# Gated linear attention started within its gates' projection, dilated attention within its values, and the stick's vector work reordered

## The chip, the cores and the metric

The kernel runs on one core of a Trainium2 chip. The metric is the time of one execution on the device, in microseconds (us). TensorE (PE) multiplies matrices; VectorE (DVE), ScalarE (ACT) and GpSimd (POOL) do everything else on tiles; SyncE (SP) and POOL start transfers. Each engine takes its instructions from a queue of its own, in a fixed order, and an instruction that waits for a semaphore holds up all that stand behind it in that queue.

## The reference

Two transformer blocks follow each other on one sequence of 512 tokens with 1024 features, all in float32. Block 1 normalises, projects with `w_in`, runs two mixers, joins them with `w_out`, and ends in a squared-relu MLP. One mixer is gated linear attention (GLA, 4 heads):

```python
glog = log_sigmoid(glow @ gla_gate_w2 + gla_gate_b) / 16
b = cumsum(glog, within chunks)                    # per channel
o = gated linear attention(q, k, v, b)             # exp(b), exp(-b) scale q and k
o_a = rmsnorm_per_head(o) * silu(gr)               # gr: the gates' projection
```

The other is dilated attention, 8 heads: softmax of `q.k + bias` over three dilated windows, joined by their log-sum-exp, times the values. Block 2 has stick-breaking attention (8 heads) and HGRN2 (4 heads of 128) side by side, then gated branches, an output projection and a SwiGLU:

```python
sp = where(causal, softplus(z), 0)                 # z = q.k / 8
w = exp(log_sigmoid(z) - (reverse cumsum(sp) - sp))
o_sb = w @ v
f = lb + (1 - lb) * sigmoid(f_in); log_f = log(f); key = 1 - f     # HGRN2
q = silu(q_in); out = hgrn2(q, key, i_in, log_f) * silu(g_in)
```

## The kernel before

Every large product is computed from split operands: a high and a low part of each (names ending in H and L: NH, NL, WH, WL), and three matmuls of 128x512 for each step over k: high by high (L660), low by high (L664), high by low (L667). One such step is called a unit here. Weights come as 128x1024 pieces into a ring of five (WH, WL): ACT rounds a piece to its high part (L1030), ACT writes the negative of that (L1038), and a transfer issued by POOL adds the raw weights to it (L2191).

The program is written as generators, one set for each engine, that yield a due time ahead of each instruction or small group. The due times are in units of PE's plan (`plan.start("qD")` is the place at which the projection qD starts); for each engine all generators are merged by due time, once, into that engine's queue. At run time only the order is left; the times themselves delay nothing.

The stages in plan order, with what matters here: the projections qG, kG, vG; the four tiles of the gate projection gG (8 units each); then the projections qD, kD, vD of dilated attention; wo0 and wo1, the two halves of `w_out`; the MLP; and in block 2 hq, hf, vH, hg, the four projections of HGRN2, beside the stick.

What the change touches:

- **GLA** (`gla` on every engine, due times from `gla_time`, which counts from `T_D`). It runs in two chunks of two heads, c=0 and c=1. PE multiplies the low-rank gate (L756); ACT takes the bank (L1099) and does abs, exp and ln (L1102, L1104, L1106); DVE finishes the logarithm (L1584) and makes three cumulative sums over 64, 128 and 256 columns (L1588, L1590, L1593); ACT takes exponentials (L1111, L1112), DVE multiplies q and k by them (L1596, L1598), and PE multiplies those (L766, a block of 16 small matmuls). Then, for 64, 128 and 256 in turn, DVE subtracts (L1604, `decay`), ACT takes two exponentials (L1116, L1117) and DVE multiplies (L1608, L1610, `values`) for PE's L777, L787 and L793. DVE masks (L1626) and PE multiplies by the values (L813).
- **The gates gG** (`silu_gates` on ACT, `silu_gate` on DVE). For each tile DVE takes it out of its bank with a scale (L1562, here called the eviction), ACT does abs, exp, ln (L954, L956, L958), DVE a step (L962), ACT an exp (L966), DVE the product (L1567). The two temporaries gT0 and gT1 take turns, and GLA's `decay` uses the same two.
- **Dilated attention** (`dilated`, due times from `T_A1` and the step `R1`). In 12 steps PE multiplies q and k (L858), DVE adds the bias and takes the row maximum (L1706), ACT takes exponentials with a sum (L1152), DVE divides (L1688, L1693), PE transposes (L846), ACT copies the bank (L1164, tile pT), and PE multiplies by the values (L833). The values' tiles of vD are taken out of their banks by ACT (L1073).
- **The stick** (`stick`, two of eight heads p=0, 1 in each step). DVE does a softplus part (L1725), the reverse scan (L1730), a difference (L1734), and for the next step a masked copy (L1746) and an abs (L1752); ACT does exp and ln (L1191, L1198, L1202) and copies the transposed weights (L1184, tile wT) for PE's L833.
- **HGRN2's gates** beside the stick: hf has the same chain as gG and ends in L1914 and L1916 on DVE and a logarithm (L1277) on ACT. `calm` gives their due times within the stick's step. vH's tiles are taken out by ACT (L1073).

## Time and profile before

| | |
|---|---|
| median of 3 runs | 1362.75 us (1362.65 to 1363.94) |
| the profiled execution | 1364.07 us |
| its span, first to last instruction | 1362.7 us |
| PE busy | 1348.6 us, 99% of the span |
| DVE busy | 873.2 us, 64% |
| ACT busy | 819.9 us, 60% |

The span is what the rows below are told in, from its start. The profiled execution is 1.3 us above the median and has 1.4 us outside its span. A busy time is the time in which an engine worked on some instruction; idle time of an engine costs only where the last engine to finish waits for it.

### The profile page before, as it was taken

Reading aid. Unit: us, or ns where it says so; the run is one execution under the profiler, and the core shown is the slowest. Engines: PE = TensorE matmul, PEld = TensorE weight load, DVE = VectorE, ACT = ScalarE, POOL = GpSimd, SP = SyncE. Lnnn points to the kernel's source line nnn. Section 1 sums busy time; section 2 is a strip of 40 time slices with the busy share of each in tenths; the row PEclk is TensorE's granted clock in tenths of the full one; section 3 lists DMA queues with packets and bytes.
Section 4 is the critical chain, followed back from the end, with each engine's and each line's share of the span. In section 5 each row is a group of like instructions: output and inputs, shape, how many; then the busy total and the mean of one; then the engine's idle time right before and its main releaser. Section 6 shows DMA issues by size and latency. Waiting matters only on the chain.

```text
span 1362.7 us, 19539 instructions
## 1 busy us (share of the span) xinstructions
PE 1348.6 (99%) x7510; PEld 1135.7 (83%) x7510; DVE 873.2 (64%) x1548; ACT 819.9 (60%) x1235; POOL 334.6 (25%) x306
## 2 busy tenths in 40 slices
PE   9999999999999999999999999999999999999999
PEld 6977956789899898887777788888888898889889
DVE  6055466577576682357787779975437785568557
ACT  6575566753544545666577767775666645754553
POOL 0211101235343251111211121211113252315214
DMA  7976643925436137876654685668888536824733
GB/s 251 238 165 144 148 117 78 231 32 196 99 98 179 33 125 191 193 169 144 149 129 111 137 217 125 137 145 182 201 214 203 110 118 194 184 47 164 188 51 109
DMA packets 57969, 202.45 MB, mean 149 GB/s; under 512 B 6450, under 2 KB 7019, under 8 KB 57748
## 3 DMA queue, kind: packets, MB, share of 16 engines
q0 software_dynamic: 25632, 93.09, 36.4%
q1 hardware_dynamic: 31380, 106.24, 23.7%
q10 hardware_dynamic: 864, 1.87, 0.4%
q8 instruction: 60, 0.98, 0.3%
q14 instruction: 33, 0.27, 0.1%
HBM read 199.05 MB, written 2.12 MB: 148 GB/s over the span
## 4 chain that ended last, share of the span: by engine, by line
PE 77%; DVE 11%; ACT 8%; DMA 3%; issue 2%; SPq 0%; POOL 0%; DVEq 0%; ACTq 0%
PE bank L660 18%; PE bank L667 18%; PE bank L664 18%; PE bank L698 17%; DVE eb L1730 2%; PE bank L813 1%; ACT WL L1038 1%; ACT eb L1198 1%; ACT WH L1030 1%; ACT zs L1152 1%; PE bank L885 1%; DVE eb L1725 1%; DMA WL<-in_w_in 1%; DMA WL<-in_w_gu 1%; DMA RAW<-in_w_in 1%
## 5 line engine op out<-in xcount | busy, mean ns | idle before, releaser
L660 PE MATMUL bank<-NH,WH 128*128 128x512 f32 x1152 | 459.8, 400 | 0.3 <-ACT NH L1207 0.3
L664 PE MATMUL bank<-NL,WH 128*128 128x512 f32 x1152 | 448.1, 390 | 0.6 <-DVE NL L1470 0.5
L667 PE MATMUL bank<-NH,WL 128*128 128x512 f32 x1152 | 448.1, 390 | 0.6 <-DVE WL L1465 0.4
L660 PEld LDWEIGHTS bank<-NH,WH 128*128 128x128 f32 x1152 | 216.5, 188 | 60.2 <-issue 17.8
L667 PEld LDWEIGHTS bank<-NH,WL 128*128 128x128 f32 x1152 | 216.2, 188 | 47.5 <-DVE WL L1465 0.8
L664 PEld LDWEIGHTS bank<-NL,WH 128*128 128x128 f32 x1152 | 216.8, 188 | 44.7 <-DVE NL L1470 1.6
L1030 ACT ACTIVATE WH<-RAW 128x1024 fp32r<-128x1024 f32 (+3 forms) x148 | 152.1, 1032 | 74.4 <-PE bank L667 39.0
L698 PE MATMUL bank<-AH,WH 128*128 128x256 f32 x644 | 182.5, 283 | 0.3 <-DVE AL L2115 0.3
L698 PE MATMUL bank<-AL,WH 128*128 128x256 f32 x644 | 182.2, 283 | 0.0
L698 PE MATMUL bank<-AH,WL 128*128 128x256 f32 x644 | 182.2, 283 | 0.0
L1038 ACT ACTIVATE WL<-WH 128x1024 fp32r<-128x1024 f32 (+1 forms) x146 | 153.3, 1052 | 12.2 <-DMA WH<-in_w_in 9.9
L2191 POOL DMA_DIRECT2D WL<-in_w_in x58 | 50.9, 889 | 318.2 <-ACT WL L1038 314.8
L698 PEld LDWEIGHTS bank<-AH,WH 128*128 128x128 f32 x644 | 123.6, 192 | 0.9 <-ACT AH L1381 0.4
L698 PEld LDWEIGHTS bank<-AL,WH 128*128 128x128 f32 x644 | 123.6, 192 | 0.2
L698 PEld LDWEIGHTS bank<-AH,WL 128*128 128x128 f32 x644 | 123.6, 192 | 0.0
L2203 POOL TENSOR_TENSOR quarters<-quarters 128x512 f32<-128x512 f32 (+1 forms) x48 | 72.2, 1503 | 128.4 <-PE bank L667 60.3
L2203 POOL TENSOR_TENSOR quarters_s<-quarters 128x512 f32<-128x512 f32 (+1 forms) x48 | 78.8, 1641 | 97.0 <-PE bank L667 51.2
L1025 ACT ACTIVATE WH<-quarters 128x1024 fp32r<-128x1024 f32 (+3 forms) x72 | 62.4, 883 | 65.0 <-PE bank L698 45.4
L1819 DVE TENSOR_TENSOR WL<-quarters,WH 128x1024 fp32r<-128x1024 f32 (+3 forms) x72 | 86.9, 1208 | 6.7 <-ACT WH L1025 6.7
L660 PE MATMUL bank<-WH,NH 128*128 128x256 f32 (+2 forms) x224 | 67.4, 308 | 2.9 <-ACT vH L1073 2.6
L1849 DVE TENSOR_TENSOR gains_hT<-gains_hT,bank 128x256 f32<-128x256 f32 x143 | 58.2, 414 | 16.2 <-PE bank L698 15.9
L667 PE MATMUL bank<-WL,NH 128*128 128x256 f32 (+2 forms) x224 | 65.1, 299 | 0.3 <-DMA WL<-in_w_in 0.3
(375 smaller groups left out, 2115.3 us busy)
## 6 DMA issues: line engine op xcount, KB each, us to landing
WL<-in_w_in POOLq DMA_DIRECT2D x58, 512.0 KB, 7.2
RAW<-in_w_gu SPq DMA_DIRECT2D x44, 512.0 KB, 5.1
WL<-in_w_gu POOLq DMA_DIRECT2D x34, 512.0 KB, 8.0
RAW<-in_w_ff SPq DMA_DIRECT2D x32, 512.0 KB, 4.6
WH<-in_w_in POOLq DMA_DIRECT2D x32, 512.0 KB, 7.1
RAW<-in_w_in SPq DMA_DIRECT2D x28, 512.0 KB, 6.4
quarters<-in_w_ff SPq DMA_DIRECT2D x24, 512.0 KB, 4.7
WL<-in_w_ff POOLq DMA_DIRECT2D x17, 512.0 KB, 6.5
```

The source lines that it names most:

```text
L660: e.matmul(o, a[0], a[1], start=(k == 0), stop=False)
L664: e.matmul(o, b[0], b[1], start=False, stop=False)
L667: mm = e.matmul(o, c[0], c[1], start=False, stop=(k == t.kt - 1))
L698: mm = e.matmul(o, a, b, start=(n in OPENS and j == 0 and i == 0), stop=(n in CLOSES and j == pairs_ - 1 and i == 2), skip_group_check=True)
L1025: e.activation(WH[p % HL][:, 0:(c if k == 3 else 2 * c)], part, ACT.Copy).then_inc(*act.sig("high", p))
L1030: e.activation(WH[p % HL][:, 0:n], RAW[raw_slot[p]][:, 0:n], ACT.Copy).then_inc(*act.sig("high", p))
L1038: e.activation(WL[p % HL][:, 0:n], WH[p % HL][:, 0:n].bitcast(F32), ACT.Copy, scale=-1.0).then_inc(*act.sig("high_negated", p))
L1730: scan = e.tensor_tensor_scan(r, r, r, 0.0, ALU.add, ALU.max)
L1819: e.tensor_tensor(WL[(p + i) % HL][:, 0:n], x, WH[(p + i) % HL][:, 0:n].bitcast(F32), ALU.subtract).then_inc(*dve.sig("low_sum", p + i))
L1849: e.tensor_tensor(hT[:, row, ts], hT[:, row, ts], bank, ALU.add).then_inc(*dve.sig("h_part", u, n))
L2191: e.dma_start(WL[p % HL][:, 0:n], src[:, k * cols:(k + m) * cols], accum_op=ALU.add).then_inc(*pool.sig(f"low_added{p % HL}", p, by=16))
L2203: e.tensor_tensor(to, a, b, op).then_inc(*pool.sig("quarter_sum", u, key))
```

## The change

It has four parts. `T_D` is 12 units earlier, so that GLA begins in the middle of gG; the gates' temporaries are then two rows of `mixed` which dilated attention fills later, and GLA's two waits for the gates are gone. `T_A1` is 4 units earlier and `R1` is 2.4 in place of 2.13, so that dilated attention begins within vD and ends where it did. In the stick each head's scan is followed at once by its difference, and each masked copy by its abs. The products of HGRN2's gates get later due times, 11.3 and 11.5 in place of 9 and 9.2 (hg: 11).

```diff
--- before.py
+++ after.py
@@ -496,8 +496,8 @@
 
             return s % 2 if bank == 0 else bank + 1
 
-        T_D = plan.start("qD")
-        T_A1, R1 = plan.start("wo0"), 3 * 0.71
+        T_D, W0 = plan.start("qD") - 12.0, plan.start("wo0")
+        T_A1, R1 = W0 - 4.0, 2.4
         T_A2, R2 = plan.start("hq") - 10.0, 4 * 2.3
         T_H, R3 = plan.start("gs"), 3.5
         ORDER = [(hp, rows) for hp in range(4) for rows in (((0, 0), (1, P)), ((2, 0),), ((3, 0),))]
@@ -548,7 +548,7 @@
             if p in after:
                 return seven_start(plan.first[after[p][0]]) + (3.0, 4.4, 12.8, 17.5, 20.2)[after[p][1]]
 
-            return plan.used[p - HL] + (1.3 if plan.used[p - HL] == T_A1 else 0.1)
+            return plan.used[p - HL] + (1.3 if plan.used[p - HL] == W0 else 0.1)
 
         def seven_start(p):
             return next(t.v0 for t in plan.tiles if t.u == plan.pieces[p][0])
@@ -1064,7 +1064,7 @@
 
             def natural(st, v, ph):
                 for t in plan.stage[st]:
-                    yield max(t.v1 + (1.4 if t.v1 == T_A1 else 1), ready_columns[ph])
+                    yield max(t.v1 + (1.4 if t.v1 == W0 else 1), ready_columns[ph])
                     j, c, bank = t.i % NT, t.i // NT, bank_for(t)
                     act.wait_ge(("product", "tile", t.g), ("scale_columns", ph))
                     if st == "vS" or st == "vH":
@@ -1272,7 +1272,7 @@
                     sigmoid_act(("hf", t.i), hk[:, t.i, :], hs[t.i % 2], freed(t), *hs_back("hf", t.i))
                     yield calm(t, 7.0)
                     sigmoid_exp(("hf", t.i), hs[t.i % 2])
-                    yield calm(t, 9.2)
+                    yield calm(t, 11.5)
                     act.wait_ge(("hf_f", t.i))
                     e.activation(hB[:, t.i, :], hs[t.i % 2], ACT.Ln).then_inc(*act.sig("hf_log", t.i))
                 return [one_(t) for t in plan.stage["hf"]]
@@ -1396,9 +1396,10 @@
 
             streams = [prologue(), ones(), splits(), negated(), root("attn", mean_time["attn"]), columns("attn", 30.0)]
             streams += [natural("vG", vG, "attn"), natural("vD", vD, "attn")]
-            streams += silu_gates("gG", lambda i: mixed[:, i, :], gt_, lambda i: [("gate", "gG", i - 2)] if i >= 2 else [])
+            streams += silu_gates("gG", lambda i: mixed[:, i, :], [mixed[:, 4, :], mixed[:, 5, :]],
+                                  lambda i: [("gate", "gG", i - 2)] if i >= 2 else [("band", i)])
             streams += [gla(0), gla(1)]
-            streams += [mixed_split("mixed", k, T_A1 - 2.0 + 0.2 * k, [("gla_out", k), ("product", "block", plan.last_unit("vD"), k)])
+            streams += [mixed_split("mixed", k, W0 - 2.0 + 0.2 * k, [("gla_out", k), ("product", "block", plan.last_unit("vD"), k)])
                         for k in range(4)]
             streams += [dilated()]
             streams += [mixed_split("mixed", k, dil_done(k - 4), [("dil_out", k - 4)]) for k in range(4, 8)]
@@ -1562,7 +1563,7 @@
                     e.tensor_tensor(o, bank_for(t), rs, ALU.mult).then_inc(*dve.sig("evac_v", t.g))
                     yield calm(t, 6.0)
                     sigmoid_dve((st, t.i), o, x)
-                    yield calm(t, 11.0 if st == "hg" else 9.0)
+                    yield calm(t, 9.0 if st == "gG" else 11.3)
                     dve.wait_ge(("sigmoid", (st, t.i)), ("evac_v", t.g))
                     e.scalar_tensor_tensor(o, o, gain(t.i), x, ALU.mult, ALU.mult).then_inc(*dve.sig("gate", st, t.i))
                 return [one_(t) for t in plan.stage[st]]
@@ -1610,11 +1611,11 @@
                     e.tensor_tensor(halves(x, m)[1], halves(d, m)[1], halves(qc, m)[1], ALU.mult).then_inc(*dve.sig("gla_x", c, m, 1))
 
                 yield gla_time(c, 5) + 0.1
-                decay(64, B64, d0, [("gla_out", 1)] if c else [("gate", "gG", 2)])
+                decay(64, B64, d0, [("gla_out", 1)] if c else [])
                 yield gla_time(c, 6)
                 values(64, d0, x64, [("gla_64", 0, 1)] if c else [])
                 yield gla_time(c, 7) + 0.1
-                decay(128, B128, d1, [] if c else [("gate", "gG", 3)])
+                decay(128, B128, d1, [])
                 yield gla_time(c, 8)
                 values(128, d1, x128_, [("gla_128", 0, 1)] if c else [])
                 dve.wait_ge(("gla_x", c, 64, 1))
@@ -1729,7 +1730,6 @@
                                 r = ee[p][:, at_:at_ + (i + 1) * P][:, ::-1]
                                 scan = e.tensor_tensor_scan(r, r, r, 0.0, ALU.add, ALU.max)
                             scan.then_inc(*dve.sig("stick_sum", s - 1, p))
-                        for p in range(2):
                             dve.wait_ge(("stick_sum", s - 1, p))
                             e.tensor_tensor(z[p], z[p], ee[p], ALU.subtract).then_inc(*dve.sig("stick_log", s - 1, p))
                     if s < NA:
@@ -1745,7 +1745,6 @@
                                 w = slice(at_, at_ + (i + 1) * P)
                                 low_ = e.tensor_tensor(z[p][:, w], FB[p][:, w], gmask[:, (3 - i) * P:S], ALU.min)
                             low_.then_inc(*dve.sig("stick_b", s, p))
-                        for p in range(2):
                             dve.wait_ge(("stick_b", s, p))
                             if s:
                                 dve.wait_ge(("stick_log", s - 1, p))
@@ -1909,7 +1908,7 @@
                     e.tensor_tensor(o, bank_for(t), rs, ALU.mult).then_inc(*dve.sig("evac_v", t.g))
                     yield calm(t, 6.0)
                     sigmoid_dve(("hf", t.i), o, f)
-                    yield calm(t, 9.0)
+                    yield calm(t, 11.3)
                     dve.wait_ge(("sigmoid", ("hf", t.i)), ("lb", 6))
                     e.tensor_scalar(f, f, olb[:, t.i:t.i + 1], lb[:, t.i:t.i + 1], ALU.mult, ALU.add).then_inc(*dve.sig("hf_f", t.i))
                     dve.wait_ge(("hf_f", t.i))
@@ -2141,9 +2140,10 @@
 
             streams = [prologue(), early_low(), sums("attn"), root("attn", mean_time["attn"]), bands(), low_rank()]
             streams += [put("qG", qG, 0.125), put("kG", kG)]
-            streams += silu_gate("gG", lambda i: mixed[:, i, :], lambda i: g_gla[:, i:i + 1], gt_, [])
+            streams += silu_gate("gG", lambda i: mixed[:, i, :], lambda i: g_gla[:, i:i + 1],
+                                 [mixed[:, 4, :], mixed[:, 5, :]], [])
             streams += [gla(0), gla(1), put("qD", qD, 0.125), put("kD", kD)]
-            streams += [mixed_split("mixed", k, T_A1 - 2.0 + 0.2 * k, []) for k in range(4)]
+            streams += [mixed_split("mixed", k, W0 - 2.0 + 0.2 * k, []) for k in range(4)]
             streams += [dilated(), to_h("wo0", "wo0", lambda k: x_in(k)[-1])]
             streams += [mixed_split("mixed", k, dil_done(k - 4), []) for k in range(4, 8)]
             streams += [to_h("wo1", "mlp", lambda k: ("h", "wo0", k)), sums("mlp")]
```

In the following pieces of the queues a line number of the changed kernel is one higher than that of the same line before, between 1400 and 1733, and one lower from 1749 on. gB and gX hold GLA's sums and products, mixed1 the gates.

DVE, from the second gate tile on, before:

```order
L962 SCALAR_TENSOR_TENSOR gT1_102<-mixed1_76,gT1_102 128x512 [waits sigmoid_a]
L1567 SCALAR_TENSOR_TENSOR mixed1_76<-mixed1_76,gains_hT_51,gT1_102 128x512 [waits evac_v,sigmoid]
L1562 TENSOR_TENSOR mixed1_76<-bank1,rs_69 128x512 [waits product]
L962 SCALAR_TENSOR_TENSOR gT0_101<-mixed1_76,gT0_101 128x512 [waits sigmoid_a]
L1581 MEMSET AT0_103 128x512 [waits masks]
L1581 MEMSET AT1_104 128x512
L1567 SCALAR_TENSOR_TENSOR mixed1_76<-mixed1_76,gains_hT_51,gT0_101 128x512 [waits evac_v,sigmoid]
L1562 TENSOR_TENSOR mixed1_76<-bank2,rs_69 128x512 [waits product]
L1584 SCALAR_TENSOR_TENSOR gB0_97<-gB0_97,gB1_98 128x512 [waits gla_a]
L1588 SCALAR_TENSOR_TENSOR gB2_99<-resets_73,gB0_97 128x512 [waits gla_vector]
L1590 SCALAR_TENSOR_TENSOR gB3_100<-resets_73,gB0_97 128x512
L1593 SCALAR_TENSOR_TENSOR gB0_97<-resets_73,gB0_97 128x512 [waits gla_vector]
```

and changed:

```order
L1563 TENSOR_TENSOR mixed1_76<-bank0,rs_69 128x512 [waits product]
L1582 MEMSET AT0_103 128x512 [waits masks]
L1582 MEMSET AT1_104 128x512
L1585 SCALAR_TENSOR_TENSOR gB0_97<-gB0_97,gB1_98 128x512 [waits gla_a]
L1589 SCALAR_TENSOR_TENSOR gB2_99<-resets_73,gB0_97 128x512 [waits gla_vector]
L962 SCALAR_TENSOR_TENSOR mixed1_76<-mixed1_76 128x512 [waits sigmoid_a]
L1591 SCALAR_TENSOR_TENSOR gB3_100<-resets_73,gB0_97 128x512
L1594 SCALAR_TENSOR_TENSOR gB0_97<-resets_73,gB0_97 128x512 [waits gla_vector]
L1568 SCALAR_TENSOR_TENSOR mixed1_76<-mixed1_76,gains_hT_51 128x512 [waits evac_v,sigmoid]
L1563 TENSOR_TENSOR mixed1_76<-bank1,rs_69 128x512 [waits product]
L1597 TENSOR_TENSOR gX0_92<-qG_80,gX0_92 128x512 [waits gla_a]
L1599 TENSOR_TENSOR gX1_93<-kG_81,gX1_93 128x512 [waits gla_a]
```

GLA's logarithm and first sum have moved ahead of the second tile's L962, and the second tile's product and the third tile's eviction now stand between GLA's sums and its products with q and k.

ACT, from GLA's bank on, before:

```order
L1099 ACTIVATE gB0_97<-bank4,gains_hT_51 128x512 [waits gla_products]
L1102 ACTIVATE gB1_98<-gB0_97 128x512 [waits gla_a]
L1104 ACTIVATE gB1_98<-gB1_98 128x512 [waits gla_a]
L1106 ACTIVATE gB1_98<-gB1_98 128x512 [waits gla_a]
L1038 ACTIVATE WL0_57<-WH0_52 128x1024 [waits high]
L954 ACTIVATE gT1_102<-mixed1_76 128x512 [waits gate,evac_v]
L956 ACTIVATE gT1_102<-gT1_102 128x512 [waits sigmoid_a]
L958 ACTIVATE gT1_102<-gT1_102 128x512 [waits sigmoid_a]
L1111 ACTIVATE gX0_92<-gB2_99 128x512 [waits gla_vector]
L1112 ACTIVATE gX1_93<-gB2_99 128x512
```

and changed:

```order
L1099 ACTIVATE gB0_97<-bank4,gains_hT_51 128x512 [waits gla_products]
L1102 ACTIVATE gB1_98<-gB0_97 128x512 [waits gla_a]
L1104 ACTIVATE gB1_98<-gB1_98 128x512 [waits gla_a]
L1106 ACTIVATE gB1_98<-gB1_98 128x512 [waits gla_a]
L966 ACTIVATE mixed1_76<-mixed1_76 128x512 [waits sigmoid_v]
L954 ACTIVATE mixed1_76<-mixed1_76 128x512 [waits gate,evac_v]
L956 ACTIVATE mixed1_76<-mixed1_76 128x512 [waits sigmoid_a]
L958 ACTIVATE mixed1_76<-mixed1_76 128x512 [waits sigmoid_a]
L1111 ACTIVATE gX0_92<-gB2_99 128x512 [waits gla_vector]
L1112 ACTIVATE gX1_93<-gB2_99 128x512
```

The second tile's exp and the whole abs, exp and ln of the third tile, which waits for that tile's eviction on DVE, now stand between GLA's logarithm and its exponentials L1111.

ACT, the exponentials of the three differences, before:

```order
L966 ACTIVATE gT1_102<-gT1_102 128x512 [waits sigmoid_v]
L1116 ACTIVATE gT0_101<-gB2_99 128x4x64 [waits gla_vector]
L1117 ACTIVATE gT0_101<-gT0_101 128x4x64
L1116 ACTIVATE gT1_102<-gB3_100 128x2x128 [waits gla_vector]
L1117 ACTIVATE gT1_102<-gT1_102 128x2x128
L1030 ACTIVATE WH1_53<-RAW1_63 128x1024 [waits product,raw1]
L1116 ACTIVATE gT0_101<-gB0_97 128x256 [waits gla_vector]
L1117 ACTIVATE gT0_101<-gT0_101 128x256
```

and changed:

```order
L1116 ACTIVATE gT0_101<-gB2_99 128x4x64 [waits gla_vector]
L1117 ACTIVATE gT0_101<-gT0_101 128x4x64
L1030 ACTIVATE WH4_56<-RAW2_64 128x1024 [waits product,raw2]
L1038 ACTIVATE WL4_61<-WH4_56 128x1024 [waits high]
L1116 ACTIVATE gT1_102<-gB3_100 128x2x128 [waits gla_vector]
L1117 ACTIVATE gT1_102<-gT1_102 128x2x128
L966 ACTIVATE mixed1_76<-mixed1_76 128x512 [waits sigmoid_v]
L1030 ACTIVATE WH0_52<-RAW0_62 128x1024 [waits product,raw0]
L1116 ACTIVATE gT0_101<-gB0_97 128x256 [waits gla_vector]
L1117 ACTIVATE gT0_101<-gT0_101 128x256
```

Two weight pieces and the third tile's exp now stand among them, one piece before the second pair, one and a half around the third.

DVE in one step of the stick, next to the first tile of hf (hs0), before:

```order
L1752 SCALAR_TENSOR_TENSOR eb0_139<-zb0_136 128x384 [waits stick_log,stick_b]
L1752 SCALAR_TENSOR_TENSOR eb1_140<-zb1_137 128x384 [waits stick_log,stick_b]
L1914 TENSOR_SCALAR hs0_143<-hs0_143,small_49 128x512 [waits constants,sigmoid]
L1916 TENSOR_SCALAR hk_147<-hs0_143 128x512 [waits hf_f]
L1725 SCALAR_TENSOR_TENSOR eb0_139<-zb0_136,eb0_139 128x384 [waits stick_l]
L1725 SCALAR_TENSOR_TENSOR eb1_140<-zb1_137,eb1_140 128x384 [waits stick_l]
L1730 SCALAR_TENSOR_TENSOR eb0_139<-eb0_139 128x128 [waits stick_sp]
L1730 SCALAR_TENSOR_TENSOR eb0_139<-eb0_139 128x256
L1730 SCALAR_TENSOR_TENSOR eb1_140<-eb1_140 128x128 [waits stick_sp]
L1730 SCALAR_TENSOR_TENSOR eb1_140<-eb1_140 128x256
L1734 TENSOR_TENSOR zb0_136<-zb0_136,eb0_139 128x384 [waits stick_sum]
L1734 TENSOR_TENSOR zb1_137<-zb1_137,eb1_140 128x384 [waits stick_sum]
```

and changed:

```order
L1746 TENSOR_TENSOR zb1_137<-bank4,cf_67 128x128 [waits stick_t,stick_z]
L1746 TENSOR_TENSOR zb1_137<-bank4,cf_67 128x256
L1751 SCALAR_TENSOR_TENSOR eb1_140<-zb1_137 128x384 [waits stick_log,stick_b]
L1726 SCALAR_TENSOR_TENSOR eb0_139<-zb0_136,eb0_139 128x384 [waits stick_l]
L1726 SCALAR_TENSOR_TENSOR eb1_140<-zb1_137,eb1_140 128x384 [waits stick_l]
L1731 SCALAR_TENSOR_TENSOR eb0_139<-eb0_139 128x128 [waits stick_sp]
L1731 SCALAR_TENSOR_TENSOR eb0_139<-eb0_139 128x256
L1734 TENSOR_TENSOR zb0_136<-zb0_136,eb0_139 128x384 [waits stick_sum]
L1731 SCALAR_TENSOR_TENSOR eb1_140<-eb1_140 128x128 [waits stick_sp]
L1731 SCALAR_TENSOR_TENSOR eb1_140<-eb1_140 128x256
L1734 TENSOR_TENSOR zb1_137<-zb1_137,eb1_140 128x384 [waits stick_sum]
L1913 TENSOR_SCALAR hs0_143<-hs0_143,small_49 128x512 [waits constants,sigmoid]
```

hf's two instructions (L1914 and L1916 before, L1913 and L1915 now) have moved from ahead of the softplus part to behind the differences, and each head's difference stands behind its own scan.

## Rows read from the trace of the kernel before

**Rows 1.** Busy time by engine, whole span: us, share, instructions.

```profile
PE 1348.6 (99%) x7510; PEld 1135.7 (83%) x7510; DVE 873.2 (64%) x1548; ACT 819.9 (60%) x1235; POOL 334.6 (25%) x306
```

**Rows 2.** Waits of PE by line and releaser: us in total, times, longest us.

```profile
PE bank L660 <- ACT vH L1073: 2.6, 4, 1.3
PE bank L846 <- DVE zs L1693: 1.6, 2, 1.1
...
PE bank L833 <- ACT wT L1184: 1.2, 1, 1.2
PE bank L858 <- DVE small L1706: 1.0, 2, 0.6
...
PE bank L833 <- ACT pT L1164: 0.6, 3, 0.3
```

**Rows 3.** Three windows: us, busy us of each engine, clock, DMA share, GB/s.

```profile
80.00:104.00 24.00, 24.00 (x130) 18.19 (x130) 14.01 (x25) 15.98 (x29) 2.94 (x4) 1.00 0.70 157
172.00:230.00 58.00, 54.63 (x376) 34.76 (x374) 37.32 (x136) 38.31 (x101) 3.46 (x4) 1.00 0.41 96
664.00:780.00 116.00, 111.96 (x703) 86.49 (x702) 91.71 (x169) 84.05 (x155) 20.95 (x29) 1.00 0.59 133
```

**Rows 4.** Timeline of PE, first GLA chunk: start us, us, instruction.

```profile
71.49 0.39 PE L660 MATMUL bank<-NH,WH 128*128 128x512 f32 x1
...
79.43 0.39 PE L667 MATMUL bank<-NH,WL 128*128 128x512 f32 x1
79.75 1.12 PE L756 MATMUL bank<-glT,gw 16*128 16x512 f32 x2
...
91.22 1.16 PE L766 MATMUL bank<-gX,gX 64*128 64x128 f32 x16
...
96.38 1.03 PE L793 MATMUL bank<-gX 64*128 64x256 f32 x4
```

**Rows 5.** Timeline of ACT in the same stretch.

```profile
73.12 0.64 ACT L966 ACTIVATE gT<-gT 128x512 f32<-128x512 f32 x1 [0.76 <-DVE gT L962]
75.17 0.63 ACT L954 ACTIVATE gT<-mixed 128x512 f32<-128x512 f32 x1 [1.42 <-DVE mixed L1562]
...
77.04 1.05 ACT L1030 ACTIVATE WH<-RAW 128x1024 fp32r<-128x1024 f32 x1
...
80.90 0.69 ACT L1099 ACTIVATE gB<-bank,gains_hT 128x512 f32<-128x512 f32 x1 [0.25 <-PE bank L756]
...
82.96 0.63 ACT L1106 ACTIVATE gB<-gB 128x512 f32<-128x512 f32 x1
...
86.29 0.62 ACT L1111 ACTIVATE gX<-gB 128x512 f32<-128x512 f32 x1
```

**Rows 6.** Timeline of DVE in the same stretch.

```profile
72.39 0.69 DVE L962 SCALAR_TENSOR_TENSOR gT<-mixed,gT 128x512 f32<-128x512 f32 x1 [2.70 <-ACT gT L958]
73.79 0.75 DVE L1567 SCALAR_TENSOR_TENSOR mixed<-mixed,gains_hT,gT 128x512 f32<-128x512 f32 x1 [0.70 <-ACT gT L966]
74.46 0.68 DVE L1562 TENSOR_TENSOR mixed<-bank,rs 128x512 f32<-128x512 f32 x1
...
83.62 0.69 DVE L1584 SCALAR_TENSOR_TENSOR gB<-gB,gB 128x512 f32<-128x512 f32 x1 [2.54 <-ACT gB L1106]
84.35 1.23 DVE L1588 TENSOR_TENSOR_SCAN gB<-resets,gB 128x512 f32<-128x512 uint8 x1
...
89.06 0.68 DVE L1598 TENSOR_TENSOR gX<-kG,gX 128x512 f32<-128x512 f32 x1
...
94.15 1.35 DVE L1626 COPY_PREDICATED AT<-resets,bank 128x512 f32<-128x512 uint8 x2
...
95.72 0.42 DVE L1610 TENSOR_TENSOR gX<-gT,qG 128x256 f32<-128x256 f32 x1
```

**Rows 7.** Timeline of DVE, the stick beside hf.

```profile
730.06 0.55 DVE L1914 TENSOR_SCALAR hs<-hs,small 128x512 f32<-128x512 f32 x1 [1.94 <-ACT hs L966]
```

**Rows 8.** Timeline of ACT, the same step.

```profile
732.13 1.06 ACT L1184 ACTIVATE wT<-bank 128x512 f32<-128x512 f32 x2
```

## Prediction

> **What bounds the kernel now.** First the busy times: PE works 1348.6 us, 99% of the span [rows 1]. The instructions of the change are the same in number and kind on every engine, so PE's own work stays as it is, and the time can change only by the 14 us in which PE stands still. Then PE's waits, grouped by what released them [rows 2]: of these stops, three kinds are those of dilated attention (zs 1.6, small 1.0, pT 0.6, together 3.2 us) and two are those of the stick beside HGRN2's projections (vH 2.6, wT 1.2, together 3.8 us). No row there names a GLA product of DVE. Then the windows [rows 3]: in the one in which GLA's first chunk runs, 80 to 104 us, PE is busy 24.00 of 24.00; dilated attention has 3.4 us of idle in 58, the stick's window 4.0 in 116; PE's clock is 1.00 in all three. So the change can win at most some 7 us in the second and third window, and in the first it can only lose. How much slack the first has is read from the timelines.
>
> **GLA's first chunk, step by step.** Before, L756 starts at 79.75 and L766, which needs the two products with q and k, at 91.22; the second product ends on DVE at 89.06 + 0.68 = 89.74 [rows 4, 6]. So 1.5 us of slack. L793 starts at 96.38, and its operand is ready at 95.72 + 0.42 = 96.14: 0.2 to 0.4 us of slack. The chain is nearly as long as the room that PE gives it.
>
> In the changed queue of PE L756 stands 36 matmuls earlier; the 36 in front of it begin at 71.49 and end with the one at 79.43, so 8.2 us [rows 4]. L756 would start at 71.6, and without stops L766 at 83.0 to 83.1, as far behind as before. Then:
>
> ACT takes the bank 1.15 us after L756 (80.90 less 79.75), at 72.7, and begins L1106 2.06 later at 74.8 [rows 5]. DVE follows 0.66 later at 75.45, and the first sum at 76.2 (84.35 less 83.62 is 0.73) [rows 6]. Up to 75.45 DVE's queue stands at GLA's logarithm. Behind it stands the second gate tile's L962, which ran at 72.39 before; it now runs at 77.3, behind the first sum (1.14 a sum with the overlap). Two more sums bring DVE to about 80.2, the second tile's product (0.67 to the next start) to 80.9, and the third tile's eviction, at 74.46 before, to 81.6 [rows 6]. Here the convoy forms: ACT's queue has that tile's abs, exp and ln ahead of GLA's two exponentials, and they can't start until 81.6. Three at 0.66 end at 83.5, the two exponentials at 84.7, and DVE's two products at 85.45. PE would want L766 at 83.1: a stop of **2.4 us**. GLA's own chain would have been ready: its first sum is there at 77.4.
>
> The same holds behind it. From L766 at 85.5 L793 is due 5.16 later (96.38 less 91.22), at 90.7. On ACT the first pair of exponentials ends at 86.6; then a weight piece rounded and negated, some 2.05 (one takes 1.05 [rows 5]), the second pair 0.8, the gate tile's exp 0.55, another piece's rounding 1.05, and the third pair 0.75: 91.8. DVE runs the tile's product, the next eviction (0.65 each) and two masks, 1.24 together from 94.15 to the next start [rows 6], after its third difference at 90.1, and has them behind it at 92.7 to 92.9; the last two products take 0.75, so 93.5 to 93.7. The stop is **2.8 us**. Both are read from fixed queues, but each waiting adds some error: 1.5 to 3.2 and 1 to 3.5.
>
> The second chunk begins within kD. No gate tile stands in it, only two evictions of 0.68 and three weight instructions of 1.05 in front of its last products. I take 0.7 (0, if its slack covers them, to 2.8, the first chunk's). Three of the L813 blocks wait for a DVE chain into which an eviction slips: 0.2 each, 0.6 (0 to 1). GLA in all: 2.4 + 2.8 + 0.7 + 0.6 = **+6.5 us**, 3 to 9.
>
> The removed waits for the gates and the separate temporaries take nothing from this: the queues' order makes the gates' work a neighbour of GLA's, whatever rows it uses. A weight piece that ACT treats 9.5 us later (L1030 at 77.04 before [rows 5], at 86.6 now) I price at nothing: it goes into a ring of five, a full round ahead of its use, and the stops above give 5 us of the 9.5 back; uncovered, PE would stop for the other 4. On SP the bias tables of dilated attention now stand ahead of two loads of raw weights; the transfer engines are busy 0.41 to 0.70 of these windows [rows 3], so this is priced at nothing too.
>
> **Dilated attention.** It begins 4 units earlier and each of the steps is 0.27 units wider, some 0.2 us of PE between the same work. The first transposes still wait for the first softmax (of the zs waits, 1.1 is one stop), since the work put ahead of them moves too: 1.1 stays. The first product with the values now has a weight piece (1.05) and the last eviction of vD in front of its copy on ACT: from a short wait to about 1.5, which is new 1.2. The later stops, 3.2 - 1.1 = 2.1, and a short one of 0.2 at the stage's start go with the wider steps. That would be -2.3 + 1.2 = **-1.1 us**, from -2.5 (nothing new) to +1 (the later stops half stay).
>
> **The stick.** Before, DVE stands idle 1.94 us in front of hf's L1914, which waits for ACT's L966, while the softplus part is queued behind it [rows 7]. The changed order puts the stick's part first. On ACT the logarithm leaves the place in front of a weight piece, so wT's copy, at 732.13 [rows 8], comes 1.0 earlier: of the 1.2 that PE waits for it 0.2 is left. Of vH's 2.6 [rows 2] three stops are large; two hang on the same DVE wait, one step later, and shrink by what DVE stood idle; the middle one is set by ACT's own row of ln, exp, weight piece, eviction, which is unchanged, and keeps most of its 0.5 idle. I leave 1.3 of 3.8: **-2.3 us** net of 0.2 for the next item, from -3.8 to -0.5, since ACT's eviction of vH stays behind the same exponentials.
>
> The turned pairs make each head's difference wait for its own scan. A dependent instruction begins 0.04 after the end of the one in front (84.35 against 83.62 + 0.69), an independent one 0.08 before it (74.46 against 73.79 + 0.75) [rows 6]: 0.12 each, two in each half step for the second head, while the first head's result is out a scan earlier. If every half step in which PE stops paid it, five, it would be 5 x 0.24 = 1.2; I take 0.2. The Trainium skill, "VectorE: DVE Perf Modes", section "The DRAIN you can't avoid", says that chained vector instructions cost the same with a semaphore after each as with one at the end, since the pipe empties in any case. By that the item would be 0 and the sum 0.2 lower; the rows just named differ by 0.12, and the measurement decides.
>
> **The sum.** +6.5 - 1.1 - 2.3 = +3.1 against the profiled execution's 1364.07: 1367.2. That execution lies 1.3 above the median of the runs, so the median becomes 1365.9.
>
> **Rivals.**
>
> *Covered start.* The gates' steps find DVE and ACT free between GLA's, because in 80 to 104 us DVE is busy only 14.0 and ACT 16.0 of 24 [rows 3], and PE keeps its 24.00 of 24.00. Decided at L766: it starts within 0.5 us of its due place. Then GLA costs 0 to 0.5, the two gains stand, and the median is 1362.75 - 3.4 + 0.3 = 1359.7: faster. Against it: the slack of 1.5 and 0.3 us and the order of the queues. The Trainium skill, "Perfetto Trace Analysis", section "Optimization Strategy", says that stages bound by different engines may gain from being interleaved. That speaks for this rival; but here the rows show PE full in the stage that is interleaved.
>
> *Half a convoy.* The first stop comes, 2.4, but it gives the later pieces room: the weight pieces don't hold the last exponentials, the second chunk is covered. GLA +3.3, sum -0.1: 1362.7, no change. For it: DVE and ACT both catch up while PE stands. Against it: L793's slack before was the smallest.
>
> *The gains don't come.* The stick's stops belong to ACT (both lines, vH and wT, are ACT's [rows 2]), and what DVE does earlier ACT does no earlier; dilated attention's stops move to its start. Sum +6.5 at most: 1369.2. For it: the releasers' names; against it: ACT's own wait for hf's product.
>
> **How the numbers follow.** The forecast as summed has 0.50, 1364.0 to 1367.8 on its own; half a convoy 0.22; covered start 0.12; no gains 0.16. A difference of 0.2%, 2.7 us, is about what a measurement of this kernel tells from none: faster is below 1360.0, slower above 1365.5. Covered start and a little of half a convoy give faster 0.13. The forecast lies 0.4 above the upper bound, so three fifths of its 0.50 are slower, with the last rival 0.46; the rest, 0.41, is no change. The range, 1361.0 to 1369.2, leaves out covered start and the upper part of the last rival.
>
> **What would show it.** In the changed profile L766 of the first chunk follows its L756 by some 13.9 us in place of 11.5, PE waits there for DVE's gX, and DVE idles some 5 us in front of the first GLA logarithm with the gate's L962 behind it; L793 of that chunk waits as well. In the window of dilated attention one stop at L833 near the start has grown and the later ones are gone. In the stick's window DVE no longer idles 1.9 us in front of hf's product and wT's wait is about 0.2. If L766 doesn't wait, the forecast is wrong in its largest term; if PE's idle in the stick's window stays near 4.0, in its second.

## The result, and the profile after

The changed kernel takes 1368.39 us (median of 12 runs, 1367.30 to 1375.37), before 1363.87 in as many: ratio 1.0042, 95% interval 1.0031 to 1.0052. It is slower, as forecast, by 4.5 us against before's 12 runs; the sum had +3.1, and it stood on the median of the three runs shown, 1362.75, 1.1 below the one of twelve. The mean granted clock is 0.993 to 0.999 in all 12 runs of the changed kernel; for before it is on record for the profiled execution and for the 59 runs beside the experiments, 1.000 in each. The profiled execution is one of the longer ones, 1373.02, at 0.996.

PE's busy time answers to [rows 1], and is 4.6 us more for the same instructions:

```profile
PE 1353.2 (99%) x7510; PEld 1138.0 (83%) x7510; DVE 877.4 (64%) x1548; ACT 818.9 (60%) x1235; POOL 334.3 (24%) x306
```

PE's waits, against [rows 2]:

```profile
PE bank L766 <- DVE gX L1599: 2.4, 1, 2.4
PE bank L787 <- DVE AT L1627: 2.1, 1, 2.1
PE bank L833 <- ACT vD L1073: 1.5, 1, 1.5
...
PE bank L846 <- DVE zs L1694: 1.2, 2, 1.0
PE bank L813 <- DVE gT L1652: 1.0, 2, 0.6
PE bank L793 <- DVE gX L1611: 0.9, 2, 0.5
PE bank L858 <- DVE small L1707: 0.8, 2, 0.4
...
PE bank L833 <- ACT pT L1164: 0.6, 2, 0.3
```

Two GLA lines now lead the list, 2.4 and 2.1 us; the stick's vH and wT have gone from it; dilated attention has a new stop of 1.5 behind the eviction of vD and keeps most of the old ones. GLA's lines together (L766, L787, L813, L793) wait 2.4 + 2.1 + 1.0 + 0.9 = 6.4 us, dilated attention's (vD, zs, small, pT) 1.5 + 1.2 + 0.8 + 0.6 = 4.1 in place of 3.2. The first GLA chunk on PE, against [rows 4]:

```profile
82.74 0.39 PE L667 MATMUL bank<-NH,WL 128*128 128x512 f32 x1
85.57 1.16 PE L766 MATMUL bank<-gX,gX 64*128 64x128 f32 x16 [2.44 <-DVE gX L1599]
...
92.39 0.68 PE L787 MATMUL bank<-gX 64*128 64x128 f32 x4 [2.13 <-DVE AT L1627]
93.54 1.31 PE L793 MATMUL bank<-gX 64*128 64x256 f32 x4 [0.47 <-DVE gX L1611]
...
95.80 0.63 PE L667 MATMUL bank<-NH,WL 128*128 128x512 f32 x1
...
105.90 0.40 PE L667 MATMUL bank<-NH,WL 128*128 128x512 f32 x1
```

L766, forecast for 85.5, stands behind a gap from 83 to 85.57, the first L787 behind another to 92.39. At 95.80 a 128x512 matmul takes 0.63 us, at 105.90 again 0.40. DVE and ACT in the same stretch, against [rows 5, 6]:

```profile
75.46 0.69 DVE L1585 SCALAR_TENSOR_TENSOR gB<-gB,gB 128x512 f32<-128x512 f32 x1 [4.68 <-ACT gB L1106]
76.18 1.22 DVE L1589 TENSOR_TENSOR_SCAN gB<-resets,gB 128x512 f32<-128x512 uint8 x1
77.33 0.67 DVE L962 SCALAR_TENSOR_TENSOR mixed<-mixed 128x512 f32<-128x512 f32 x1
...
80.95 0.68 DVE L1563 TENSOR_TENSOR mixed<-bank,rs 128x512 f32<-128x512 f32 x1
84.17 0.69 DVE L1597 TENSOR_TENSOR gX<-qG,gX 128x512 f32<-128x512 f32 x1 [2.54 <-ACT gX L1111]
...
90.26 0.74 DVE L1568 SCALAR_TENSOR_TENSOR mixed<-mixed,gains_hT 128x512 f32<-128x512 f32 x1
90.92 0.68 DVE L1563 TENSOR_TENSOR mixed<-bank,rs 128x512 f32<-128x512 f32 x1
91.52 1.32 DVE L1627 COPY_PREDICATED AT<-resets,bank 128x512 f32<-128x512 uint8 x2
...
93.08 0.41 DVE L1611 TENSOR_TENSOR gX<-gT,qG 128x256 f32<-128x256 f32 x1
```

```profile
81.66 0.63 ACT L954 ACTIVATE mixed<-mixed 128x512 f32<-128x512 f32 x1 [3.01 <-DVE mixed L1563]
...
83.53 0.61 ACT L1111 ACTIVATE gX<-gB 128x512 f32<-128x512 f32 x1
```

This is the convoy of the forecast: DVE idle 4.68 us in front of GLA's logarithm, the second gate tile's L962 behind it at 77.33, the third tile's eviction at 80.95, and on ACT that tile's L954, which waited 3.01 us for it, ahead of GLA's L1111, whose input had been there since 77.4. Behind the first stop the gate's product and eviction (90.26, 90.92) and the masks (91.52) stand on DVE ahead of GLA's last product. L787 writes a bank that the first mask gives back, so it waits for the mask; L793 waits for the last product. Then the windows (us, busy us of PE, PEld, DVE, ACT, POOL, clock), against [rows 3]:

```profile
84.00:94.00 10.00, 5.83 (x47) 4.45 (x48) 8.08 (x18) 8.73 (x17) 1.73 (x2) 1.00 0.46 97
94.00:106.00 12.00, 12.00 (x38) 8.48 (x37) 2.15 (x4) 2.93 (x9) 0.00 (x0) 0.57 0.41 95
177.00:236.00 59.00, 54.78 (x382) 36.64 (x381) 33.83 (x127) 37.74 (x97) 3.46 (x4) 1.00 0.49 116
670.00:787.00 117.00, 116.47 (x727) 91.01 (x726) 100.73 (x177) 85.64 (x158) 21.97 (x31) 1.00 0.61 140
```

From 94 to 106 us the clock is 0.57 on average, most of that time at the lower of its two levels (1.2 and 2.4 GHz); the stops lie ahead of it. By that row 12 x (1 - 0.57) = 5.2 us of PE's work were lost there. In the stick's window PE idles 0.5 us in place of 4.0.

To see where time comes and goes, the start of the same product matmul (L660, L664, L667, counted in order) in two traces can be compared. The table shows by how much each kernel falls further behind before's profiled execution in four stretches, named by before's time (negative: it gets ahead):

| kernel | up to 60 us | 60 to 266 (GLA, dilated) | 663 to 769 (stick) | the rest |
|---|---|---|---|---|
| changed | 0.0 | +12.7 | -4.6 | +0.9 |
| GLA alone | -0.3 | +7.6 | 0.0 | +0.5 |
| all but GLA | +0.6 | +2.0 | -4.6 | +0.9 |
| gates behind | +0.5 | +4.1 | -4.5 | +0.4 |
| filler | +0.1 | +8.1 | -4.5 | +2.1 |
| stick alone | +0.8 | -0.1 | -4.6 | +0.7 |
| later products alone | -0.4 | -0.1 | -5.1 | -0.7 |
| turned pairs alone | +0.1 | +0.9 | +4.9 | +1.3 |
| dilated alone | +2.3 | +2.0 | 0.0 | -0.5 |
| temporaries alone | -0.4 | -0.1 | 0.0 | +0.3 |
| before, once more | -0.8 | -0.1 | 0.0 | -0.5 |

The last row is the same program as the reference: without any edit, its first column differs by 0.8 and its last by 0.5 us.

### The profile page after: what moved, and what is told of

Read it like the earlier page. It is cut to its first block, busy times and chain, and to the rows that moved or that the text cites. A ratio compares the mean times of both kernels' runs of the same rounds, so it can differ in the third digit from the quotient of the medians.

```text
span 1371.7 us, 19544 instructions
## 1 busy us (share of the span) xinstructions
PE 1353.2 (99%) x7510; PEld 1138.0 (83%) x7510; DVE 877.4 (64%) x1548; ACT 818.9 (60%) x1235; POOL 334.3 (24%) x306
## 4 chain that ended last, share of the span: by engine, by line
PE 76%; DVE 12%; ACT 6%; issue 3%; DMA 2%; SPq 0%; POOL 0%; DVEq 0%; ACTq 0%; POOLq 0%
PE bank L660 18%; PE bank L667 18%; PE bank L664 18%; PE bank L698 16%; DVE eb L1731 2%; PE bank L813 1%; DVE eb L1726 1%; PE bank L885 1%; DMA WL<-in_w_in 1%; ACT WH L1030 1%; ACT WL L1038 1%; ACT zs L1152 1%; DVE zb L1746 1%; DVE zb L1734 1%; DMA RAW<-in_w_in 1%
## 5 line engine op out<-in xcount | busy, mean ns | idle before, releaser
L660 PE MATMUL bank<-NH,WH 128*128 128x512 f32 x1152 | 460.7, 401 | 0.4 <-ACT NH L1207 0.2
L664 PE MATMUL bank<-NL,WH 128*128 128x512 f32 x1152 | 448.8, 391 | 0.5 <-DVE NL L1471 0.5
L667 PE MATMUL bank<-NH,WL 128*128 128x512 f32 x1152 | 448.9, 391 | 0.5 <-DVE WL L1466 0.5
L660 PEld LDWEIGHTS bank<-NH,WH 128*128 128x128 f32 x1152 | 216.6, 188 | 61.6 <-issue 19.8
L667 PEld LDWEIGHTS bank<-NH,WL 128*128 128x128 f32 x1152 | 216.7, 188 | 47.4 <-DVE WL L1466 0.9
L664 PEld LDWEIGHTS bank<-NL,WH 128*128 128x128 f32 x1152 | 216.8, 188 | 44.5 <-DVE NL L1471 2.3
L660 PE MATMUL bank<-WH,NH 128*128 128x256 f32 (+2 forms) x224 | 66.8, 305 | 0.4 <-DVE kS L1900 0.3
L667 PE MATMUL bank<-WL,NH 128*128 128x256 f32 (+2 forms) x224 | 65.1, 299 | 0.3 <-DMA WL<-in_w_in 0.3
```

The lines of the kernel that those rows point to most:

```text
L660: e.matmul(o, a[0], a[1], start=(k == 0), stop=False)
L664: e.matmul(o, b[0], b[1], start=False, stop=False)
L667: mm = e.matmul(o, c[0], c[1], start=False, stop=(k == t.kt - 1))
```

## The experiments

In the cuts of code here `...` stands for what is left out, and the comments are added. **GLA alone** (against before; so are all whose name says alone):

```diff
-        T_D = plan.start("qD")
+        T_D = plan.start("qD") - 12.0
-... silu_gates("gG", ..., gt_, lambda i: [("gate", "gG", i - 2)] if i >= 2 else [])
+... silu_gates("gG", ..., [mixed[:, 4, :], mixed[:, 5, :]], ... if i >= 2 else [("band", i)])
-                decay(64, B64, d0, [("gla_out", 1)] if c else [("gate", "gG", 2)])
+                decay(64, B64, d0, [("gla_out", 1)] if c else [])
...                                                  # decay(128) and DVE's silu_gate likewise
```

> Only GLA's earlier start, with the gates' temporaries in free rows; dilated attention and the stick as before. If the loss is GLA's convoy and the clock that falls behind it: L766 and L787 of the first chunk stop for about 2.5 us each as in the changed kernel, the granted clock falls to half for some us behind them, and the time is 6 to 10 us over before (ratio 1.0045 to 1.007). If the loss came from elsewhere (dilated attention or the tail), this kernel is within 3 us of before.

1372.91 us, ratio 1.0076 (1.0058 to 1.0093), +8.9: GLA is the loss. The clock is 0.995 to 0.998 in its 6 runs. Its trace holds something the expectation hadn't:

```profile
85.23 1.17 PE L766 MATMUL bank<-gX,gX 64*128 64x128 f32 x16 [2.45 <-DVE gX L1599]
...
87.35 0.63 PE L667 MATMUL bank<-NH,WL 128*128 128x512 f32 x1
...
92.67 0.90 PE L787 MATMUL bank<-gX 64*128 64x128 f32 x4
93.40 1.03 PE L793 MATMUL bank<-gX 64*128 64x256 f32 x4
```

```profile
86.00:94.00 8.00, 8.00 (x40) 5.91 (x37) 6.79 (x16) 7.90 (x15) 1.73 (x2) 0.57 0.64 135
94.00:104.00 10.00, 10.00 (x49) 7.66 (x49) 2.52 (x4) 5.36 (x10) 0.00 (x0) 1.00 0.44 104
```

Here the clock fell right behind the first stop, and PE at the lower level arrived at L787 so late that it didn't wait there. L793 stands at 93.40, in the changed kernel at 93.54: PE's speed between the two stops made no difference here, because the chain on ACT and DVE sets the second. Most of the +7.6 of this trace are thus 3.9 us of stops (L766, L793, L813) and 8 x (1 - 0.57) = 3.4 at the lower clock, which stand in the place of the stop at L787. In the changed kernel's profile the clock fell during L793, between 94 and 95, where nothing covers it.

**All but GLA**: the changed kernel with T_D, the temporaries and the waits of before.

```diff
-        T_D, W0 = plan.start("qD") - 12.0, plan.start("wo0")
+        T_D = plan.start("qD")
+        W0 = plan.start("wo0")
...                                                  # temporaries and waits as before
```

> The whole change but GLA's: its start and its temporaries are those of before. If GLA is the whole loss: the clock stays at 1.00 between 80 and 110 us, PE has no stop there, and the time is 2 to 4 us below before (ratio 0.997 to 0.9985), the stick's gain of about 3.5 less or plus 1 for dilated attention. If the other parts cost as well, it is at before or over it.

1361.44, ratio 0.9985 (0.9976 to 0.9993), -2.6, all clocks 1.000. As expected, with the two parts of opposite sign: +2.0 and -4.6 in the table. The two runs don't add up to the whole: +8.9 - 2.6 = +6.3 where the changed kernel has +4.5; four of its 12 runs have a mean clock of 0.999, none of GLA alone's. Nor does each stop bring the clock down: in this kernel's trace PE stops 1.5 and 1.2 us at the start of dilated attention, and all 11 runs have 1.000.

**Gates behind**: the changed kernel, with other due times for the second to fourth gate tile (`late`).

```diff
-                yield calm(t, 2.0)                     # ACT, abs, exp, ln
+                yield calm(t, 2.0) if late in (0, 1, False) else gla_time(0, 0) + (0, 0, 12.9, 18.6)[t.i]
-                    yield due(t)                       # DVE, eviction
+                    yield gla_time(0, 0) + (0, 0, 7.1, 16.6)[t.i] if late in (2, 3) else due(t)
-                    yield calm(t, 6.0)                 # DVE, L962; the exp and the product likewise
+                    yield gla_time(0, 0) + (0, 6.9, 16.8, 21.8)[t.i] if late else calm(t, 6.0)
```

> The changed kernel, with the gate work of the second to fourth tile of gG put behind GLA's products on DVE and ACT (the third and fourth evictions too). If the queues' order is the cause: L766 starts within 0.5 us of its due place, 11.5 us behind L756, the stop at L787 shrinks below 1 us, the clock doesn't fall, and the time is 5 to 8 us below the changed kernel, so 0 to 3 us below before. If it is the density of the work itself that is the cause, both stops stay over 1.5 us and the time stays within 2 us of the changed kernel.

L766 doesn't wait any more; what is left in GLA:

```profile
PE bank L813 <- DVE gT L1654: 1.0, 2, 0.6
PE bank L793 <- DVE gX L1613: 1.0, 2, 0.5
...
PE bank L787 <- DVE AT L1629: 0.8, 1, 0.8
```

So the order of the queues made the first stop. But the time is 1368.07 (ratio 1.0021, 1.0011 to 1.0030), and it is two times: 4 runs of 11 with a clock of 1.000 take 1363.5 to 1365.1, 7 with 0.996 to 0.998 take 1368.0 to 1369.7. The expectation that the clock would stay, and with it that of 5 to 8 us below the changed kernel, was wrong. The trace is of one of the four runs without a fall; its stops in GLA are 0.4 to 0.8 us each. What stops the other seven had, and where their clock fell, no trace shows.

**Filler**: the changed kernel, with matmuls whose result nothing reads.

```diff
+                if c == 0:                                     # in front of L766
+                    for _ in range(10):
+                        e.matmul(OB, NH[:, 0, 0:P], NH[:, 0, :], start=True, stop=True)
...
+                    if c == 0 and hh == 0:                     # in front of the first L787
+                        for _ in range(9):
+                            e.matmul(OB, NH[:, 0, 0:P], NH[:, 0, :], start=True, stop=True)
```

> The changed kernel, with 10 matmuls of 128x512 that nothing reads in front of L766 and 9 in front of the first L787 of the first chunk, 2.3 and 2.0 us of PE work in the place of the two stops. If the clock falls because PE stood still: the clock stays at 1.00 there, the stops of the engines behind are unchanged, and the time is 1 to 4 us below the changed kernel in the same runs, with mean clocks of 1.00. If the clock falls for another reason (the form of the small matmuls), it still falls and the time is the changed kernel's or above it.

```profile
83.08 2.43 PE L762 MATMUL bank<-NH 128*128 128x512 f32 x10
85.70 1.16 PE L769 MATMUL bank<-gX,gX 64*128 64x128 f32 x16 [0.19 <-DVE gX L1605]
...
90.23 2.23 PE L790 MATMUL bank<-NH 128*128 128x512 f32 x9
...
93.70 1.13 PE L799 MATMUL bank<-gX 64*128 64x256 f32 x4 [0.47 <-DVE gX L1617]
```

```profile
PE bank L891 <- DVE ATh L1671: 1.6, 1, 1.6
```

```profile
94.00:106.00 12.00, 12.00 (x58) 9.32 (x57) 3.01 (x5) 7.11 (x14) 0.87 (x1) 1.00 0.51 119
```

The clock is 1.00 in the profile and in all 5 runs; in its trace GLA and dilated attention cost 8.1 in place of 12.7. So it falls because PE stands still there, and the difference, 4.6, is the clock's part in the changed kernel's profiled execution (5.2 by the window's clock). The expected gain in time did not come: 1369.04 (ratio 1.0034, 1.0022 to 1.0046) is +5.0 over before, the changed kernel +4.5. L766 and L793 start where they did, and in this trace a wait far behind, L891 (L885 in the changed kernel), takes 1.6 us in place of 0.3; whether it does in all five runs is not shown. The changed kernel's profile is one of its longer executions; in a usual one, with a higher mean clock, the clock's part must be smaller, and these runs don't say how large it is.

**Behind, with filler**: gates behind, with 3 and 2 such matmuls in front of L787 and L793 of the first chunk, 1 and 2 in the second.

> The kernel with the gate work behind GLA's products, with 3 and 2 matmuls that nothing reads in the two stops left in the first chunk, and 1 and 2 in the second, 0.2 to 0.7 us each place. In the runs without them 7 of 11 had a mean clock of 0.996 to 0.998 and took 1368 to 1370, 4 had 1.000 and took 1363.5 to 1365.1. If short stops of PE are what makes the clock fall: 1.000 in nearly all runs and 1364 to 1366. If not: the two kinds of runs stay.

1364.77 (ratio 1.0006, 0.9997 to 1.0015); 10 of 11 runs at 1.000 and 1363.5 to 1365.0, one at 0.999 and 1367.9. The second kind of run has nearly gone, with work of under 2 us that does nothing. That speaks for the short stops at L787 and L793. But gates behind ran on another chip and was not run again beside this one, so that the chip made the difference is not excluded (before has 1.000 on both).

**Temporaries alone**: T_D of before, the rest of GLA's edits.

> Only the gates' temporaries in two free rows, and the two waits for the gates gone; GLA starts where it did. If the rows and waits take no part in the loss: within 1 us of before, PE without a stop in GLA's first chunk and its clock at 1.00. If they do (the waits had kept DVE's queue in step): 1 to 3 us over.

1364.33 against 1364.06, ratio 1.0002 (0.9993 to 1.0012). No part in it.

**Stick alone, later products alone, turned pairs alone**:

```diff
-                    yield calm(t, 11.0 if st == "hg" else 9.0)      # later products: hq, hg; hf and
+                    yield calm(t, 9.0 if st == "gG" else 11.3)      # its logarithm likewise
...
-                        for p in range(2):                          # turned pairs: scan, difference
                             dve.wait_ge(("stick_sum", s - 1, p))
...
-                        for p in range(2):                          # and copy, abs
                             dve.wait_ge(("stick_b", s, p))
```

> Only the stick's part: the turned pairs and the later due times of HGRN2's gate products. In the changed kernel PE's matmuls gain 4.6 us over before between 727 and 769 us of before's trace, where I forecast 2.3. If that gain is the stick's own: PE's idle in that stretch falls from 4.0 to about 0.5 us, and the time is 4 to 5 us below before (ratio 0.9965). If it came only because the earlier stops of the changed kernel had put the stages out of step: 1 to 2.5 us below before.

> Only the later due times of HGRN2's gate products and hf's logarithm, the pairs of the stick as before. By my forecast this is the whole gain, since the turned pairs only add 0.12 us each: 4 to 5 us below before, the same as or slightly better than with the turned pairs. If the turned pairs carry part of it: 2 to 3 us below before.

> Only the turned pairs (each head's scan followed by its difference, each masked copy by its abs). By my forecast 0 to 1 us over before. If they carry part of the gain, by giving the first head's result a scan earlier to ACT: 1.5 to 2.5 us below before, with shorter waits of PE for vH and wT.

1359.57 (0.9964, 0.9951 to 0.9976), **1358.29** (0.9953, 0.9940 to 0.9965) and 1369.19 (1.0037, 1.0024 to 1.0049). The later products alone are the best kernel of the study, 5.8 us below before. DVE in the step of [rows 7], later products alone:

```profile
727.16 1.00 DVE L1734 TENSOR_TENSOR zb<-zb,eb 128x384 f32<-128x384 f32 x2
728.08 0.54 DVE L1914 TENSOR_SCALAR hs<-hs,small 128x512 f32<-128x512 f32 x1
```

L1914 stands behind the difference and waits for nothing. The turned pairs cost 5.1 us by themselves and 1.3 beside the later products. One step of them, and the same step before:

```profile
674.50 1.03 DVE L1725 SCALAR_TENSOR_TENSOR eb<-zb,eb 128x384 f32<-128x384 f32 x2 [1.00 <-ACT eb L1202]
675.44 1.00 DVE L1730 TENSOR_TENSOR_SCAN eb<-eb 128x128 f32<-128x128 f32 x2
676.48 0.56 DVE L1733 TENSOR_TENSOR zb<-zb,eb 128x384 f32<-128x384 f32 x1
676.95 1.00 DVE L1730 TENSOR_TENSOR_SCAN eb<-eb 128x128 f32<-128x128 f32 x2
677.99 0.56 DVE L1733 TENSOR_TENSOR zb<-zb,eb 128x384 f32<-128x384 f32 x1
...
681.67 0.56 DVE L1725 SCALAR_TENSOR_TENSOR eb<-zb,eb 128x384 f32<-128x384 f32 x1 [0.40 <-ACT eb L1202]
```

```profile
673.21 1.03 DVE L1725 SCALAR_TENSOR_TENSOR eb<-zb,eb 128x384 f32<-128x384 f32 x2 [1.00 <-ACT eb L1202]
...
679.84 0.56 DVE L1725 SCALAR_TENSOR_TENSOR eb<-zb,eb 128x384 f32<-128x384 f32 x1 [0.40 <-ACT eb L1202]
```

From one softplus part to the next it is 7.17 us here and 6.63 before. Each difference starts 0.04 after its scan ends, as priced; with copy and abs there are four such places in a step, 4 x 0.12 = 0.48 of the 0.54 us. The loop over DVE and ACT takes every step's delay into the next one. PE shows it late: at 715 us of before's time this kernel has lost 0.2 us since 663, at 727 it has lost 3.4, part of it stops of PE, part a stretch at the lower clock behind them (0.83 from 725 to 735 us of its own time).

**Dilated alone**:

```diff
-        T_A1, R1 = plan.start("wo0"), 3 * 0.71
+        W0 = plan.start("wo0")
+        T_A1, R1 = W0 - 4.0, 2.4
```

> Only dilated attention's earlier start and wider steps, GLA as before. My forecast for this part was 1.1 us less. The traces of the changed kernel (lag unchanged over the stage, +0.1) and of the one without GLA's shift (+2.0) say: 1 to 2.5 us over before, with a stop of 1.5 at the first product with the values behind ACT's eviction of vD, and one of 1.2 at GLA's last product with the gates, which stands beside it when GLA has not moved.

1365.77 (1.0013, 1.0004 to 1.0022), +1.7:

```profile
PE bank L834 <- ACT vD L1074: 1.5, 1, 1.5
...
PE bank L661 <- DVE mixed L1656: 1.2, 1, 1.2
```

Both stops are there: the copy of vD, and the one at GLA's end, which the changed kernel, where GLA ends earlier, doesn't have. **Best try** kept T_A1 = W0 with 2.4, and had the later products:

> HGRN2's gate products later, as in the run with these alone (5.8 us below before), and dilated attention with the wider steps of 2.4 but started where before starts it, so that its first product with the values and GLA's last one are not met. If the later stops of dilated attention go with wider steps: another 1 to 2 us, 7 us below before (ratio 0.995). If wider steps only push its end into the second half of w_out: at 5 us below before or less.

1359.72 (0.9968, 0.9955 to 0.9980): 4.3 us below before and slower than the later products alone, so the second of the two expectations came. The steps' waits shrink, but one of 0.9 for the split of dilated attention's output appears in the second half of `w_out`.

**Before, once more**:

> The kernel before, once more, for what differs between two executions of the same program. The other traces are all 0.6 to 0.9 us behind before's in the last 20 us (a wait of PE for gains_hT) and 0 to 2.3 at 50 us (a weight transfer). If that is chance: this execution shows one or both as well. If it is the changes': neither.

1362.59. It has neither, which would speak for the changes. But the kernel with the stick's part alone, whose edits lie behind 660 us, is 0.8 behind at 60 us, and the one with the temporaries alone, whose edits lie before 170 us, has the late wait, while the later products alone and the best try have not. Neither goes with one edit, and one trace of a kernel can't tell more: a difference of about a microsecond in the first and last columns of the table, and the 2.3 in dilated alone's first, are not put down to any edit here.

## Why the prediction was right in its direction and wrong in its size

- GLA's stops were forecast rightly, in order and length: +6.5 forecast, 6.4 us of waits on its lines measured. In the first chunk 2.4 and 2.8 were forecast, and 2.4 and 2.1 + 0.5 came; for the second chunk and the L813 blocks 0.7 and 0.6 were forecast, and 0.5 and 1.0 came. Up to L766 DVE's and ACT's events lie within about 0.1 us of the times worked out. Only the place was off: most of the second stop came one block earlier, at L787, which needs a bank back from DVE's mask, a link that the prediction did not have. The half convoy and the covered start are refuted.
- The step that failed is the one ahead of **the sum**, that "PE's own work stays as it is, and the time can change only by the 14 us in which PE stands still". Every stop was then taken at its own length, and the cost of TensorE's clock, 1.00 in the three windows before, was no term. In the profiled execution PE is busy 4.6 us longer with the same instructions: the clock cost 4.6 to 5.2 us behind the stops. In a usual run it cost less: the four runs with a mean of 0.999 take 1367.3 to 1368.5, the two with 0.993 take 1374.1 and 1375.4. A fall that comes early costs nothing where the chain on ACT and DVE holds PE up in any case, as in GLA alone.
- Dilated attention's **-1.1** has the wrong sign: its waits are 0.9 us more in the changed kernel, and it costs 2.0 in the trace of the run alone, where GLA's end is met as well. The stop forecast at 1.5 came at 1.5; of the later stops, 2.1 us that wider steps were to take away, 1.6 stayed. This half of the rival "the gains don't come" was right.
- The stick's gain of **-2.3** is -4.6. I left 1.3 us of stops that are gone, and took each stop at its idle time alone: PE's idle time in the stretch falls by 3.5. It is the later products' gain, 5.8 by the medians; the item "turned pairs", 0.2, is 1.3 beside them and 5.1 alone. I priced it per stop of PE, where it counts per step of a loop. The rule of the Trainium skill that I weighed against it ("VectorE: DVE Perf Modes", "The DRAIN you can't avoid"), by which it would be nothing, is not borne out here: the rows show 0.12 for each place, and the run without the turned pairs is 1.3 us faster. The same section of the Trainium skill excepts a next instruction that is not held, which starts earlier; that agrees with the 0.08 of overlap in [rows 6].
- That the sum came near is partly luck: the misses of dilated attention (+2.0) and the stick (-2.3) nearly cancel. With the sizes of the traces it would be 6.4 + 0.9 - 4.6 = +2.7. Measured are 4.5 between the medians. The 1.8 left is of the size of the clock's part in a usual run (an estimate: a mean of 0.998 is 0.002 x 1368 = 2.7 us of PE's work), but the filler runs, at 1.000, are no faster, so how it is shared between the clock and waits elsewhere stays open.

## What to carry to other kernels

Where TensorE is busy 99% of the time, price a new stop of it not at its length alone but with the chance that its clock falls behind it. The kernel with two stops of 2.1 to 2.4 us had a lowered clock in every run, and matmuls that do nothing in their place took that away; stops of under a microsecond seem to have done it in some runs, while stops of 1.5 and 1.2 us in dilated attention did not. What decides between them is not shown. When a chain is started earlier, write the changed queues of the helper engines side by side: work that was next to nothing becomes the neighbour in front. And price an order of two engines that feed each other by the step of their loop, not by the stops that the bound engine shows today.

## What the runs showed of the hardware that was not expected

The clock's fall is not the same in each execution of one program: the changed kernel's 12 runs have mean clocks of 0.993 to 0.999, and 4 of 11 runs of gates behind had no fall. Nor is its place: in the profile of GLA alone the slower matmuls lie between 86.3 and about 93 us, behind the first stop, in the changed kernel's between about 94.5 and 105, behind the second. At the lower level a 128x512 product follows the one before it by 0.427 us in place of 0.227 (changed kernel, at 100 to 102 us against 79 to 80).
